# Second feed-forward's up-projection: weights as the moving operand, with a return path over VectorE transposes and SBUF to SBUF transfers

## Chip, cores and metric

One core of a Trainium2 chip. The metric is the device time of one execution in microseconds, as the median of three runs.

## What is computed

A sequence of 256 tokens of width 2048 goes through two transformer blocks, all in fp32. The change touches only the last part, the gated feed-forward of the second block, with 2 x 5632 hidden channels and a causal convolution of three taps over the tokens. Cut to what matters:

```
hn  = rms_norm(h, g2)                            # 256 x 2048
u   = hn @ w_up                                  # 256 x 11264: for each of 5632 channels a gate and a value
u   = w0*u[t-2] + w1*u[t-1] + w2*u[t]            # per channel, over tokens
a   = silu(u_gate) * u_value                     # 256 x 5632
out = h + rms_norm(a @ w_down, g3)               # 256 x 2048
```

## The kernel before

**Weights.** All weights of the program lie in one array `wstream` of 756 pieces. A piece is 512 KB, eight blocks of 128x128. SP loads them in order into a ring of four slots (`raw`); the load of piece i waits until the low part of piece i-4 has been made (`lo_ready`). Every product is made of three, for precision: a weight is split into a high part (ScalarE, `split_hi`, L1802, which waits until TensorE has used the piece four before it, `piece_used`) and a low part (VectorE, `split_lo`, L1100), and the activations have a high and a low part too (`A[:, k, 0]`, `A[:, k, 1]`; `H` likewise). High x high, high x low and low x high are summed in PSUM.

**Stages.** The second feed-forward runs in three chunks of 16, 16 and 12 tiles of 128 hidden channels (`CHUNKS2`). Each chunk has an up stage (`up0`, `up1`, `up2`: 64, 64 and 48 pieces) and a down stage (`dn0`, `dn1`, `dn2`: 32, 32 and 24 pieces). The stages follow each other without a break on TensorE; ScalarE and VectorE prepare pieces up to three ahead of it.

**Up stage.** The function `units` (L486, L494) takes four units (128 channels each; gate and value of two tiles) in turn. A weight block is the stationary operand. With its high part 512 columns go through (`A[:, k, :, :]`, both parts of 256 tokens), with its low part 256 columns. The result stands in PSUM with channels on partitions: 256 columns and 256 more, which VectorE adds up (`tensor_reduce`, L1131) into `z`, one unit every two pieces. GpSimd scales it by the norm's factor into `ub` (L2257), ScalarE makes the first tap (`c0`, L2207), VectorE the two others (`conv`, L1721 and L1724), ScalarE the sigmoid (L2213), GpSimd two products (L2341, L2347), ScalarE the high part of H (L2216), GpSimd the low part (L2352, `up_ready`). Within a chunk H tile i follows two units.

**Down stage.** In `down2` (L1059 to L1061) activations are stationary: for each of the tiles k and both halves of the tokens three matmuls of 512 columns, into two banks, one for each half. The four column groups f come one after another; each needs all H tiles.

**Opening of up0.** The norm ahead of up0 is made half by half: `turn_half` and `next_tiles` transpose tiles of x on TensorE (L958, L1014), ScalarE and VectorE make the parts of A (`a4_ready`, L1678, L1689), and the first two pieces are done by `half_piece` (L975, L981) for each token half by itself; `spread_rs` (L527) spreads the norm's factor over the partitions.

Of the kernel before, what the change touches and what calls it, by code (L numbers as in the profile page):

```python
# [26 lines left out]
P = 128  # L27
S = 256
# [43 lines left out]
for _c, _n in enumerate(CHUNKS2):  # L72
    STAGES += [(f"up{_c}", 2 * _n, 16), (f"dn{_c}", 8, _n)]
# [4 lines left out]
NZ = {"gate": 0, "wo": 0, "fd0": 0, "fd1": 0, "fd2": 0, "fd3": 0, "vs": 0, "cv": 0, "v2": 0, "misc": 1, "proj": 0, "wo2": 0, "dn0": 0, "dn1": 0, "dn2": 0}  # L78
_p = _u = _z = 0
for _name, _n, _k in STAGES:  # L80
    PB[_name], UB[_name], ZB[_name] = _p, _u, _z
    _blocks = _n * _k
    if _name in ("vs", "v2"):
        _blocks = _n // 2 * 4 * 16
    if _name[:2] in ROWS:
        _blocks = 16 * _k
    _p += 1 if _name == "misc" else _blocks // BLK
    _u += _n
    _z += NZ.get(_name, _n)
# [17 lines left out]


BY_TILE = tuple((k, k + 1) for k in range(12)) + ((12, 14, 0), (14, DT, 0), (12, 14, 2), (14, DT, 2))
# [43 lines left out]
ATT_PIECES = 32 + len(WO_FIRST)  # L153

# [39 lines left out]
def program(nc, xT, pT, wstream, consts, setup, params, grows, xrows, out):  # L194
# [11 lines left out]
    with ExitStack() as ctx:  # L206
# [47 lines left out]
        ub, c0 = ring(ptf, 0, 4, S + 4), ring(ptf, 4 * (S + 4), 2)  # L254
# [31 lines left out]
        mask = con[:, CO["mask"][0]:CO["mask"][1]]  # L286
        rs2b, rs3 = vN[:, QT, 0:S], vN[:, QT, S:2 * S]
# [61 lines left out]
        half_turned, post_half_hi, post_half_lo = sem("half_turned"), sem("post_half_hi"), sem("post_half_lo")  # L349
        up_c0, up_step, up_conv, up_sig, up_gated, up_h, up_hi, up_ready = (  # L350
# [71 lines left out]
        def _(sp):  # L422
# [11 lines left out]
            def load(i, s):  # L434
                sp.wait_ge(lo_ready, i - SLOTS + 1)
                sp.dma_start(raw[:, s, :], wstream[ds(i, 1)].rearrange("a p n -> p (a n)")).then_inc(raw_landed[s], 16)

            with sp.Fori(1, NPIECE // SLOTS - 1) as it:
                for j in range(SLOTS):
                    load(it * SLOTS + (SLOTS + j), j)  # L440
            for i in range(NPIECE // SLOTS * SLOTS, NPIECE):
                sp.wait_ge(lo_ready, i - SLOTS + 1)
                sp.dma_start(raw[:, i % SLOTS, :], wstream[i]).then_inc(raw_landed[i % SLOTS], 16)
# [10 lines left out]
        def _(pe):  # L454
# [74 lines left out]
            def rows_group(p, p0, u, u0, K, src, ready=None, between={}, upper=False):  # L529
# [4 lines left out]
                for k in range(K):  # L534
# [426 lines left out]
            def half_piece(q, t, js, between=None):  # L961

                p, tok = PB["up0"] + q, slice(t * P, t * P + P)
                pe.wait_ge(lo_ready, p + 1)
                blocks = [(k, j) for k in (2 * q, 2 * q + 1) for j in js]
                for k, j in blocks:
                    if t:
                        pe.wait_ge(a4_ready, k + 1)
                    else:
                        pe.wait_ge(post_half_lo, k + 1)  # L970
                        if k == 0:
                            pe.wait_ge(z_ready, UB["up0"] + j + 1)
                    i = (k % 2 * 4 + j) * P
                    bank = psum[(UB["up0"] + j) % 4][:, :].rearrange("p (h c) -> p h c", h=2)
                    nc.tensor.matmul(bank[:, :, tok], whi[:, p % SLOTS, i:i + P], A[:, k, :, tok], start=(k == t == 0), stop=False)  # L975
                if between:
                    between()
                for k, j in blocks:
                    i = (k % 2 * 4 + j) * P
                    bank = psum[(UB["up0"] + j) % 4][:, tok]  # L980
                    last = nc.tensor.matmul(bank, wlo[:, p % SLOTS, i:i + P], A[:, k, 0, tok], start=False, stop=False)  # L981
                if t:
                    last.then_inc(piece_used, 1)
# [40 lines left out]
            for q in range(2):  # L1024
                half_piece(q, 0, range(3))
            turn_half(1)
            for q in range(2):
                half_piece(q, 0, range(3, 4))
            half_piece(0, 1, range(4))
            half_piece(1, 1, range(4), between=lambda: next_tiles(0))  # L1030
# [3 lines left out]
            for c, n in enumerate(CHUNKS2):  # L1034
                up, dn = f"up{c}", f"dn{c}"

                def hidden2(it, **more):
                    units(it * 8 + PB[up], PB[up], it * 4 + UB[up], UB[up], 4, DT, lambda j, k: A[:, k, :, :],
                          lambda k: (a4_ready, k + 1), **more)
                if c == 0:  # L1040
                    late = {q: lambda q=q: next_tiles(q) for q in range(2, 6)}
# [4 lines left out]
                def down2(it, f):  # L1046

                    p = it * n + f * n // 2 + PB[dn]
                    s0 = PB[dn] + f * n // 2
                    u, u0 = it * 4 + 2 * f + UB[dn], 2 * f + UB[dn]  # L1050
                    for t in range(QT):
# [1425 lines left out]
```

## Time and profile before

| | us |
|---|---|
| runs, median of 3 | 2211.14 |
| runs, lowest and highest | 2210.64, 2211.28 |
| profiled execution, span | 2209.0 |
| TensorE busy | 2197.2 (99%) |
| VectorE busy | 1445.2 (65%) |
| ScalarE busy | 1106.9 (50%) |
| GpSimd busy | 550.7 (25%) |
| DMA, mean | 188 GB/s |

The span goes from the first to the last instruction of the profiled execution. Busy times of engines overlap each other. A matmul's shown duration (389 ns for 512 columns) is longer than the distance between two of them, since they are pipelined; the rate of TensorE is read from the starts in the timeline.

### The profile page before, as it was taken

To read this page: it belongs to the slowest core of one execution; us is meant where nothing else is said; L and a number is where in the kernel's file an instruction comes from. 1 tells how busy PE (TensorE), PEld (TensorE's weight loads), DVE (VectorE), ACT (ScalarE), POOL (GpSimd) and SP (SyncE) were. 2 spreads that over 40 slices of the span, in tenths; PEclk is the share of its full clock that TensorE was granted. 3 is DMA by queue.
4 is the path that set the end of the run, shared out by engine and by line. 5 is a ranking of instruction groups with operands and counts; after the bars stand their busy time and mean duration, and the time that the engine had idled before them with its cause. 6 is when DMAs were issued, how large, how long until landed. Compare 5 with 4: busy or idle time off the path is not lost.

```text
span 2209.0 us, 34195 instructions
## 1 busy us (share of the span) xinstructions
PE 2197.2 (99%) x11625; PEld 1878.9 (85%) x11625; DVE 1445.2 (65%) x1925; ACT 1106.9 (50%) x1654; POOL 550.7 (25%) x531
## 2 busy tenths in 40 slices
PE   9999999999999999999999999999999999999998
PEld 7888988888888888888888887888888888888887
DVE  6877765555664565555566667567785688756875
ACT  6445555453453454445455455565553455534553
POOL 3202220350240141053000033005540245403431
PEclk9999999999999999999999999999999999999999
DMA  7675335556555555556555653545555555555554
GB/s 254 232 230 163 115 128 204 170 190 208 191 190 192 189 189 192 186 192 193 187 185 179 227 171 135 193 160 188 195 188 196 192 183 192 189 195 192 186 209 149
DMA packets 118072, 414.21 MB, mean 188 GB/s; under 512 B 12896, under 2 KB 18048, under 8 KB 117472
## 3 DMA queue, kind: packets, MB, share of 16 engines
q1 hardware_dynamic: 111600, 401.37, 53.9%
q10 hardware_dynamic: 6384, 11.70, 1.7%
q8 instruction: 52, 0.85, 0.2%
q14 instruction: 36, 0.29, 0.0%
HBM read 409.29 MB, written 2.15 MB: 186 GB/s over the span
## 4 chain that ended last, share of the span: by engine, by line
PE 98%; DVE 1%; ACT 1%; issue 0%; DMA 0%; DVEq 0%; ACTq 0%
PE bank L486 33%; PE bank L494 17%; PE bank L543 7%; PE bank L545 7%; PE bank L544 7%; PE bank L1059 4%; PE bank L1060 4%; PE bank L1061 4%; PE bank L599 1%; PE bank L601 1%; PE bank L600 1%; PE bank L619 1%; PE bank L994 1%; PE bank L656 1%; PE bank L796 1%; PE bank L798 1%
## 5 line engine op out<-in xcount | busy, mean ns | idle before, releaser
L1100 DVE TENSOR_TENSOR wboth<-raw,wboth 128x1024 fp32r<-128x1024 f32 x756 | 982.2, 1302 | 607.8 <-ACT wboth L1802 607.1
L1802 ACT CAST wboth<-raw 128x1024 fp32r<-128x1024 f32 x756 | 790.9, 1049 | 711.5 <-PE bank L545 241.6
L486 PE MATMUL bank<-A,wboth 128*128 128x512 f32 x2928 | 705.1, 391 | 0.3 <-DVE wboth L1100 0.3
L486 PEld LDWEIGHTS bank<-A,wboth 128*128 128x128 f32 x2928 | 537.0, 188 | 104.6 <-issue 1.0
L494 PEld LDWEIGHTS bank<-A,wboth 128*128 128x128 f32 x2928 | 376.7, 191 | 14.8
L494 PE MATMUL bank<-A,wboth 128*128 128x256 f32 x2928 | 384.0, 283 | 0.0
L543 PE MATMUL bank<-wboth,H 128*128 128x512 f32 x576 | 224.6, 390 | 0.0
L545 PE MATMUL bank<-wboth,H 128*128 128x512 f32 x576 | 224.2, 389 | 0.0
L544 PE MATMUL bank<-wboth,H 128*128 128x512 f32 x576 | 224.1, 389 | 0.0
L2257 POOL TENSOR_TENSOR bias<-z,rs 128x256 f32<-128x256 f32 x64 | 75.7, 1182 | 481.2 <-DVE z L1131 391.6
L2257 POOL TENSOR_TENSOR PT<-z,rs 128x256 f32<-128x256 f32 x88 | 73.4, 835 | 465.4 <-DVE z L1131 464.8
L1131 DVE TENSOR_REDUCE z<-bank 128x256 f32<-128x512 f32 x172 | 118.2, 688 | 41.1 <-PE bank L486 40.8
L1059 PE MATMUL bank<-wboth,H 128*128 128x512 f32 x352 | 136.9, 389 | 0.0
L1060 PE MATMUL bank<-wboth,H 128*128 128x512 f32 x352 | 136.9, 389 | 0.0
L1061 PE MATMUL bank<-wboth,H 128*128 128x512 f32 x352 | 136.9, 389 | 0.0
L545 PEld LDWEIGHTS bank<-wboth,H 128*128 128x128 f32 x576 | 108.1, 188 | 22.6
L543 PEld LDWEIGHTS bank<-wboth,H 128*128 128x128 f32 x576 | 108.1, 188 | 22.3
L544 PEld LDWEIGHTS bank<-wboth,H 128*128 128x128 f32 x576 | 108.1, 188 | 22.2
L2347 POOL TENSOR_TENSOR bias<-Sm 128x256 f32<-128x256 f32 x44 | 70.0, 1592 | 37.9 <-DVE Sm L1724 37.7
L486 PE MATMUL bank<-H,wboth 128*128 128x512 f32 x320 | 79.1, 394 | 0.0
L2010 ACT ACTIVATE Sm<-bias 128x256 f32<-128x256 f32 x64 | 26.8, 418 | 102.6 <-POOL bias L2257 102.6
L1061 PEld LDWEIGHTS bank<-wboth,H 128*128 128x128 f32 x352 | 66.1, 188 | 13.8
(293 smaller groups left out, 2409.1 us busy)
## 6 DMA issues: line engine op xcount, KB each, us to landing
raw<-wstream SPq DMA_DIRECT2D x756, 512.0 KB, 3.3
bias<-bias_rows ACTq DMA_DIRECT2D x6, 512.0 KB, 5.4
x<-xrows ACTq DMA_DIRECT2D x1, 2048.0 KB, 10.0
bias<-grows ACTq DMA_DIRECT2D x2, 1024.0 KB, 6.1
out<-x SPq DMA_DIRECT2D x8, 256.0 KB, 2.1
x<-xT SPq DMA_DIRECT2D x7, 256.0 KB, 4.6
pA<-bias_rows ACTq DMA_DIRECT2D x2, 512.0 KB, 8.9
Sm<-grows ACTq DMA_DIRECT2D x1, 1024.0 KB, 5.8
```

The source lines that it names most:

```text
L486: last = nc.tensor.matmul(bank(j)[:, :], whi[:, s, cols(i)], moving(j, k), start=(k == 0), stop=(k == K - 1))
L494: last = nc.tensor.matmul(bank(j)[:, 0:S], wlo[:, s, cols(i)], moving(j, k)[:, 0, :], start=False, stop=False)
L543: nc.tensor.matmul(bank[:, :], src[:, k, 0, tok], whi[:, s, w], start=(k == 0), stop=False)
L544: nc.tensor.matmul(bank[:, :], src[:, k, 0, tok], wlo[:, s, w], start=False, stop=False)
L545: last = nc.tensor.matmul(bank[:, :], src[:, k, 1, tok], whi[:, s, w], start=False, stop=(k == K - 1))
L1059: nc.tensor.matmul(bank[:, :], H[:, k, 0, tok], whi[:, s, w], start=(k == 0), stop=False)
L1060: nc.tensor.matmul(bank[:, :], H[:, k, 0, tok], wlo[:, s, w], start=False, stop=False)
L1061: return nc.tensor.matmul(bank[:, :], H[:, k, 1, tok], whi[:, s, w], start=False, stop=(k == n - 1))
L1100: V.tensor_tensor(wlo[:, s, :], raw[:, s, :], whi[:, s, :].bitcast(F32), ALU.subtract).then_inc(lo_ready, 1)
L1131: V.tensor_reduce(dst(j) if dst else z[:, (z0 + j) % 4, :], bank[:, :].rearrange("p (h c) -> p c h", h=2), AX, ALU.add).then_inc(z_ready, 1)
L1802: C.copy(whi[:, s, :], raw[:, s, :]).then_inc(hi_ready, 1)
L2257: return lambda zz: G.tensor_tensor(dst, zz, by, ALU.mult)
```

## The change

In up stages the activations become the stationary operand and 512 columns of weights (four units) the moving one; the code is the existing `rows_group`. A group of four units takes eight pieces, and its result stands in two banks with tokens on partitions and 4 x 128 channels in the columns. To bring it back to channels on partitions, VectorE transposes each bank in blocks of 32x32 into `flip` (`up_flip`; the buffer of `z`), which keeps each block in its quarter of 32 partitions, and 16 transfers of 32 partitions x 1 KB on the SP queue carry the blocks from quarter i to quarter j (`carry`, into `land`, two buffers in `kT`). GpSimd reads `land`, scales and writes `ub` as before. The taps, products and splits of a group of four come at fixed places of the piece order (`TAP_AT`, `CONV_AT`, `GATE_AT`, `HIGH_AT`), 12 to 16 pieces after the group's first piece. In SP's order the six, five and five transfers of a group stand ahead of three successive loads (`CARRY`, `LOADED`).

In the down stages the pieces of the first two column groups are interleaved (`dn_first`): all but the last two of f=0, then all but the last two of f=1, then the two last of each. The weight stream is laid out accordingly. The opening of up0 uses `half_tiles`, tile by tile for each half. Loops over up and down stages are written out.

```
-    STAGES += [(f"up{_c}", 2 * _n, 16), (f"dn{_c}", 8, _n)]
+    STAGES += [(f"up{_c}", _n, 16), (f"dn{_c}", 8, _n)]
+LOADED = 7
+TAP_AT, GATE_AT, HIGH_AT = (12, 12, 13, 13), (13, 14), (15, 16)
+CONV_AT = (12, 12, 13, 14)
+CARRY = [range(0, 6), range(6, 11), range(11, 16)]
+def dn_first(n):
+    return [(f, h) for f in range(2) for h in range(n // 2 - 2)] + [(f, h) for f in range(2) for h in (n // 2 - 2, n // 2 - 1)]
+        flip = z[:, :, :].rearrange("p a b -> p (a b)")
+        land = [kT[:, i, :, :].rearrange("p a b -> p (a b)")[:, 0:8 * P] for i in range(2)]
...
+            def carry(src, dst, steps_of, landed):
+                for step in steps_of:
+                    i, j = divmod(step, 4)
+                    sp.dma_start(dst[32 * j:32 * j + 32, 256 * i:256 * i + 256],
+                                 src[32 * i:32 * i + 32, 256 * j:256 * j + 256]).then_inc(landed, 16)
+            def up_carry(c, m, steps_of):
+                if 0 in steps_of:
+                    sp.wait_ge(z_ready, 4 + UB[f"up{c}"] + 2 * m + 2)
+                    if c or m >= 2:
+                        sp.wait_ge(z_used, 4 + ZB[f"up{c}"] + 4 * m - 4)
+                carry(flip, land[m % 2], steps_of, up_landed)
+            done = BLK
+            for c, n in enumerate(CHUNKS2):
+                p = PB[f"up{c}"] + LOADED
+                loads(done, p)
+                for i in range(4 * n + 4):
+                    for step, part in enumerate(CARRY):
+                        if i - step >= 8 and (i - step) % 8 == 0:
+                            up_carry(c, (i - step) // 8 - 1, part)
+                    load(p + i, (p + i) % SLOTS)
...
+            half_tiles((0, 1), 0)
+            half_tiles((2,), 0)
             turn_half(1)
+            half_tiles((3,), 0)
+            half_tiles((0, 1), 1)
+            half_tiles((2,), 1)
+            next_tiles(0)
+            half_tiles((3,), 1)
             next_tiles(1)
...
-                    hidden2(0, mixed=1, first=BY_TILE, begin=2, halved=(6,), between={**late, NORM_AT["up0"]: lambda: spread_rs(3)})
-                with pe.Fori(1 if c == 0 else 0, n // 2) as it:
-                    hidden2(it)
+                for m in range(n // 2):
+                    rows_group(PB[up] + 8 * m, PB[up] + 8 * m, UB[up] + 2 * m, UB[up] + 2 * m, DT, A, lambda k: (a4_ready, k + 1), late,
+                               begin=4 if c == m == 0 else 0)
...
+                for i, (f, h) in enumerate(dn_first(n)):
+                    dn_piece(PB[dn] + i, f, h)
...
+            def up_flip(c, m):
+                dve.wait_ge(piece_used, PB[up] + SLOTS + 8 * m + 8)
+                if c or m:
+                    dve.wait_ge(up_landed, 64 * (ZB[up] - ZB["up0"] + 4 * m))
+                for t in range(QT):
+                    V.transpose(flip.rearrange("p (j t d b) -> p t d j b", j=4, t=QT, d=4)[:, t, :, :, :],
+                                psum[(UB[up] + 2 * m + t) % 4][:, :].rearrange("p (d j a) -> p d j a", d=4, j=4)).then_inc(z_ready, 1)
...
+                for m in range(n // 2):
+                    pool.wait_ge(up_landed, 64 * (ZB[up] - ZB["up0"] + 4 * m + 4))
+                    for j in range(4):
+                        preact(4 * m + j)
+                    for i in (2 * m, 2 * m + 1):
+                        gated(i)
+                        product(i)
+                    for i in (2 * m, 2 * m + 1):
+                        product_lo(i)
```

## Rows read from the trace of the kernel before

**Rows 1.** The page's first line: span of the profiled execution.
```profile
span 2209.0 us, 34195 instructions
```

**Rows 2.** The page's chain of work that ended last, by engine.
```profile
PE 98%; DVE 1%; ACT 1%; issue 0%; DMA 0%; DVEq 0%; ACTq 0%
```

**Rows 3.** Windows: busy time of each engine in up1.
```profile
core 0: us, PE busy (x) PEld busy (x) DVE busy (x) ACT busy (x) POOL busy (x), PEclk, DMA share, GB/s
1737.00:1915.00 178.00, 178.00 (x1025) 157.33 (x1024) 144.66 (x159) 94.31 (x126) 83.39 (x76) 1.00 0.55 187
```

**Rows 4.** Timeline of TensorE, up0 and start of dn0: start, duration, instruction, count.
```profile
1559.03 3.82 PE L486 MATMUL bank<-A,wboth 128*128 128x512 f32 x16
1562.68 2.08 PE L494 MATMUL bank<-A,wboth 128*128 128x256 f32 x16
1564.60 3.82 PE L486 MATMUL bank<-A,wboth 128*128 128x512 f32 x16
...
1648.09 2.00 PE L486 MATMUL bank<-A,wboth 128*128 128x512 f32 x8
1649.93 0.39 PE L1059 MATMUL bank<-wboth,H 128*128 128x512 f32 x1
```

**Rows 5.** Timeline of TensorE: first matmuls of up1.
```profile
1736.97 1.98 PE L486 MATMUL bank<-A,wboth 128*128 128x512 f32 x8
```

**Rows 6.** Source line L543, gate stage: duration ns min/median/max, first and last start.
```profile
L543 PE MATMUL bank<-wboth,A x128: 389/389/476, 1112.5 to 1202.5; 128*128 128x512 f32 x128
```

**Rows 7.** Timeline of TensorE in the opening of up0.
```profile
1464.64 0.87 PE L975 MATMUL bank<-A,wboth 128*128 128x256 f32 x6
...
1486.21 0.60 PE L1014 MATMUL bank<-con,x 128*128 128x128 f32 x4
...
1489.94 0.70 PE L527 MATMUL bank<-acc,ones 128*128 128x256 f32 x2 [0.33 <-DVE acc L1190]
```

**Rows 8.** Timeline of VectorE in the opening of up0.
```profile
1466.65 0.75 DVE L1673 SCALAR_TENSOR_TENSOR x<-y,small,x 128x512 f32<-128x512 f32 x1
...
1470.59 1.22 DVE L1100 TENSOR_TENSOR wboth<-raw,wboth 128x1024 fp32r<-128x1024 f32 x1
1471.73 0.74 DVE L1673 SCALAR_TENSOR_TENSOR x<-y,small,x 128x512 f32<-128x512 f32 x1
1472.88 0.88 DVE L1678 SCALAR_TENSOR_TENSOR A<-bank,par,A 128x256 fp32r<-128x256 f32 x2 [0.41 <-ACT A L2140]
```

**Rows 9.** Groups by line in up1, dn1 and up2; last, source line L2257.
```profile
L1100 DVE TENSOR_TENSOR wboth<-raw,wboth 128x1024 fp32r<-128x1024 f32 x144 | 196.1, 1362 | 78.2 <-ACT wboth L1802 78.2
L1802 ACT CAST wboth<-raw 128x1024 fp32r<-128x1024 f32 x144 | 151.4, 1052 | 128.0 <-PE bank L1061 51.7 <-PE bank L494 45.0 <-PE bank L486 31.3
L1721 DVE SCALAR_TENSOR_TENSOR Sm<-PT,par 128x256 f32<-128x256 f32 x55 | 40.1, 729 | 0.0
L1131 DVE TENSOR_REDUCE z<-bank 128x256 f32<-128x512 f32 x55 | 38.0, 691 | 17.9 <-PE bank L486 17.9
L1724 DVE SCALAR_TENSOR_TENSOR Sm<-PT,par,Sm 128x256 f32<-128x256 f32 x55 | 26.7, 485 | 2.0
...
L2257 POOL TENSOR_TENSOR PT<-z,rs x88: 732/740/1785, 1493.3 to 2136.7; 128x256 f32<-128x256 f32 x88
```

**Rows 10.** Source line L1745: copy of 512 PSUM columns on VectorE.
```profile
L1745 DVE COPY y<-bank x8: 680/686/694, 1672.0 to 1737.9; 128x512 f32 x8
```

**Rows 11.** Transfers: issues by line, KB, us to landing; durations of two issues, ns.
```profile
raw<-wstream SPq DMA_DIRECT2D x756, 512.0 KB, 3.3
out<-x SPq DMA_DIRECT2D x8, 256.0 KB, 2.1
vT<-vT ACTq DMA_DIRECT2D x1, 256.0 KB, 5.4
...
L436 SPq DMA_DIRECT2D raw<-wstream x748: 332/333/823, 17.2 to 2179.3; - x187
L1972 ACTq DMA_DIRECT2D vT<-vT x1: 487/487/487, 166.8 to 166.8; - x1
```

More of the change, by code:

```diff
@@ L86 @@
         _blocks = 16 * _k
+    if _name[:2] == "up":
+        _blocks = 2 * _n * _k
     _p += 1 if _name == "misc" else _blocks // BLK
@@ L435, in load, with loads @@
                 sp.wait_ge(lo_ready, i - SLOTS + 1)
[L436 to L443, printed above, removed]
+                piece = wstream[i] if isinstance(i, int) else wstream[ds(i, 1)].rearrange("a p n -> p (a n)")
+                sp.dma_start(raw[:, s, :], piece).then_inc(raw_landed[s], 16)
+            def loads(a, b):
+                with sp.Fori(a // SLOTS, b // SLOTS) as it:
+                    for j in range(SLOTS):
+                        load(it * SLOTS + j, j)
+                for i in range(b // SLOTS * SLOTS, b):
+                    load(i, i % SLOTS)
+            def carry(src, dst, steps_of, landed):
[18 more added lines that the diff above has]
+                    load(p + i, (p + i) % SLOTS)
+                done = p + 4 * n + 4
+            loads(done, NPIECE)
             for t in range(QT):
@@ L533, in rows_group @@
                         pe.wait_ge(z_ready, u + t + 1)
-                for k in range(K):
+                for k in range(begin, K):
                     if ready:
@@ new lines, in _ @@
+                for i in range(n, 2 * n):
+                    if n == CH or i < 3 * n // 2 + FIN_SPLIT // 2:
+                        dn_piece(PB[dn] + i, 2 * i // n, i % (n // 2))
+                t0 += n
+            p = PB["dn2"] + 3 * n // 2
+            for t in range(QT):
+                for k in range(FIN_SPLIT, n):
+                    pe.wait_ge(lo_ready, p + k // 2 + 1)
+                    last = rows_of(p + k // 2, 3, k, t)
+                    if t and k % 2:
+                        last.then_inc(piece_used, 1)
+                if t == 0:
+                    last.then_inc(dn_half, 1)
@@ new lines, in down2_in @@
+            def down2_in(c, f):
+                dn, n = f"dn{c}", CHUNKS2[c]
+                last = dn_first(n).index((f, n // 2 - 1)) if f < 2 else n // 2 * f + n // 2 - 1
+                dve.wait_ge(piece_used, PB[dn] + SLOTS + last + 1)
+                for t in range(QT):
+                    dst = yN[:, t, f * WIDE:f * WIDE + WIDE]
+                    bank = psum[(UB[dn] + 2 * f + t) % 4][:, :]
+                    if c == 0:
+                        V.tensor_copy(dst, bank).then_inc(z_ready, 1)
+                    else:
+                        V.tensor_tensor(dst, dst, bank, ALU.add).then_inc(z_ready, 1)
@@ L2431 @@
     for n in CHUNKS2:
-        stream += [ordered(both[t0:t0 + n].reshape(2 * n, DT, P, P), 1 if t0 == 0 else 0, first=BY_TILE), rows(down[t0 * P:(t0 + n) * P])]
+        wide = both[t0:t0 + n].reshape(n // 2, 4, DT, P, P).transpose(0, 2, 1, 3, 4).reshape(-1, P, P)
+        stream += [wide, rows_out(down[t0 * P:(t0 + n) * P], dn_first(n))]
         t0 += n
```

239 lines of the change are left out of this document (89 added, 150 removed).

## Prediction

> **What bounds the kernel now.** I read the chain that ended last first: 98% of the span is TensorE [rows 2]. The windows by stage say the same of the second feed-forward: in the 178 us of up1 TensorE is busy for all 178, VectorE for 145, ScalarE 94, GpSimd 83, at a granted clock of 1.00 and a DMA share of 0.55 [rows 3]. So only two things can move the time here: what TensorE takes for a piece of weights, and new waits of TensorE. The timeline gives the first. In a regular up stage two pieces (16 wide matmuls of 512 columns, 16 narrow ones of 256) repeat; the block at 1559.03 comes again at 1564.60, and the sixteenth repeat starts at 1648.09: 89.06 us for 32 pieces, 2.783 us a piece [rows 4]. Inside it the wide run starts at 1559.03 and the narrow one at 1562.68, 3.65/16 = 0.228 us a wide one; 1562.68 to 1564.60 is 0.120 us a narrow one. Half the columns cost more than half the time, by about 6 ns here, so each matmul carries some 13 ns that its columns don't explain. A down stage has 12 matmuls of 512 columns a piece, activations stationary: dn0 starts at 1649.93, up1 at 1736.97, 87.04 us for 32 pieces, 2.720 us a piece [rows 4, 5].
>
> **Part 1, the matmuls.** Per piece the old up stage streams 8x512 + 8x256 = 6144 columns in 16 matmuls, the new one 12x512 = 6144 in 12. The columns are equal; four matmuls fewer at 13 to 16 ns are the 0.063 us between 2.783 and 2.720. I price a new up piece at the down stage's 2.720, since its loop is `rows_group`, the code that also runs the gate stage with A as the stationary operand; there a matmul shows the same 389 ns [rows 6] as in the down stages. Up1 and up2 have 64 + 48 = 112 pieces: 112 x 0.0631 = 7.1 us off, all of it on the path.
>
> Up0 has 64 pieces in 1464.64 to 1649.93 = 185.29 us [rows 4, 7]. Its last seven groups, 56 pieces, become 152.3 us. The first group has to be laid out step by step, as it is fed by the norm, whose VectorE and ScalarE work isn't changed. TensorE does three tiles of token half 0, 3 x 0.68 = 2.04 us, to 1466.7, then wants the transposes of half 1; the VectorE step that they read (the one at 1466.65, 0.75 long) ends at 1467.4 [rows 8]: 0.7 us of waiting that is new, because the old code had 2.8 us of matmuls ahead. Then 0.4 of transposes, tile 3, and tiles 0 to 2 of half 1 to 1470.6, as the halves arrive from 1468.5 on; transposes 0.35, tile 3, transposes 0.35, to 1472.05. Tile 4 needs a weight split at 1470.59 (1.22), an add at 1471.73 (0.74) and a 0.44 us low part: ready at 1472.9 [rows 8], a second wait of 0.85. Pieces 2 to 5 and three sets of transposes bring TensorE to 1484.8; the fourth set starts there. In the trace that set starts at 1486.21 and the matmul that spreads the norm's factor at 1489.94 [rows 7], 3.73 later, all VectorE and ScalarE. The same 3.73 gives 1488.6, while TensorE is done with piece 6 at 1487.9: a third wait of 0.7. Then 0.35 + 2.72: group 0 ends at 1491.6, 27.0 us. Up0 is 27.0 + 152.3 = 179.3, 6.0 us less. The down stages keep their matmuls, only reordered: 0.
>
> **Part 2, from PSUM back to channels on partitions.** Four reductions a group of 8 pieces (691 ns each) go; two 512-column transposes come, which no row shows. Nearest is the copy of 512 PSUM columns, 0.69 us [rows 9, 10]; as the low end I take 0.35 (a half), as the high end the 1.36 us of a 1024-column split, since a strided write could be slow. VectorE then has, a group, 8 x 1.36 + 4 x (0.73 + 0.49) + 2 x 0.69 = 17.1 us of TensorE's 21.8; 18.5 at the high end. It is not the bound, and its two transposes are back to back where four reductions were spread, so one low part comes 1.4 us later; three split pieces (8.2 us) lie ahead of TensorE then. The price is 0, beyond this cover the excess.
>
> **Part 3, sixteen 32 KB transfers a group on SP.** This queue also issues the weight loads. What is queued behind: the first six transfers wait for the transposes, and behind them stands the load of piece 8m+15; five more stand before 8m+16, five before 8m+17. An issue takes 0.333 us; one of ScalarE, from SBUF to SBUF, 0.487 [rows 11]. Let E be the end of a group on TensorE. Transposes done at E+1.4, six issues to E+3.6, the load, five issues; the next load waits for the low part of piece 8m+12, at E + 2.72 + 1.05 + 1.36 = E+5.1; the last five are out at E+7.3 to E+8. TensorE wants piece 8m+15 at E+19.0, and its high and low part take 1.05 + 1.36 [rows 9], so the first must start by E+16.6, and the load, 3.3 us from issue to landing [rows 11], must go by E+13: 9 us of cover. The loads behind it have as much. The last transfer lands 2.1 us (out from x) to 5.4 us (SBUF to SBUF, 256 KB) after its issue [rows 11], at E+10 to E+13. ScalarE looks for it after the high part of piece 8m+15, at E + 4 x 2.72 + 1.05 = E+12, holding only splits that TensorE wants by E+21.8, so it may be late until about E+16. GpSimd's four scalings (740 to 1785 ns each [rows 9]) run behind it. Price 0; 22 x the excess beyond E+16. The bytes: 512 KB more for every 4 MB, so the share of 0.55 goes to 0.62, or 0.68 if 1 KB rows cost double; no bound.
>
> The Trainium skill (DMA: Bandwidth & Descriptors, section on measured HBM to SBUF transfers) says that transfers below 64 KB are dominated by their descriptors, and speaks against this. Its 0.95 us of DMA time at 64 KB would, if the sixteen were served one after another, make an estimate of 15 us, to E+16.6, stall every group by 0.6 us and bring the time back to 2211; no run here shows it. The mechanism is rival (b) below.
>
> **Part 4, the seams.** The last group's H comes late: gate and copy are placed 13 to 16 pieces after the group's start, the last convolution runs behind the low part of piece 8m+17 (E + 6 x 2.72 + 2.41 = E+18.7) to about E+20.5, the product to E+22, ScalarE's last copy behind the split of piece 8m+19 (E+22.8) to E+23.2, and GpSimd's two low parts are done at about E+23.5 and, at 0.74 to 1.79 each, E+24 to E+25.6. The reordered down stage asks for it at its piece 13 (E+35) with 16 tiles and at piece 9 (E+24.5, second tile E+25.9) with 12: no wait in chunks 0 and 1; in chunk 2 0 to 1.5 us, I take 0. Without the reordering all three seams would stall, by 6 us (piece 7, E+19) or 11 us (piece 5, E+13.6). The tail behind the last matmul isn't touched.
>
> **Sum.** 6.0 + 7.1 = 13.1 us. Span 2209.0 [rows 1] - 13.1 = 2195.9. The median of the runs lies 2.1 above the span; this adds to 2198.0. Bounds: without the three waits of group 0, 2195.8; with 1.5 us at the seam and a group 0 no shorter than before, 2202.
>
> **Rivals.** (a) The return path is late by a little in each group (slow scatter of the transposes, 32 KB transfers landing at E+17 or so): 0.1 to 0.4 us x 22 takes back 2 to 9 us, 2200 to 2207. Against it: 3 us of cover even at the 5.4 us landing. (b) Slower than before, by one mechanism: the transfers are served in series in the queue, each holding the next. At 2.1 us each [rows 11] sixteen end at E+35, 19 us past the deciding point of E+16, and 22 groups lose some 400 us; it decides from (16 - 1.4)/16 = 0.9 us a transfer, and at 1.0 us it costs 22 x 1.4 = 31 us: 2229. Against it: the eight output transfers at the end are issued closer than their 2.1 us landing and still show 2.1 to 2.2 each, so they overlap. (c) The change doesn't do what it says, as the 0.063 us belongs to the mixture of high and low parts and not to the count: then up pieces stay at 2.78 and the time at 2211. The gate stage speaks against it. (d) Group 0 is better than laid out, with no waits: 2196.
>
> **How the numbers follow.** Forecast 2198.0, from 2195.5 to 2201: 0.70, with (d) inside. (a) 0.14, of which 0.03 ends within 0.2% (4.4 us, about what a measurement of this kernel can tell from no change). (b) 0.08; (c) 0.05; better than 2195.5, 0.03. Faster 0.70 + 0.11 + 0.03 = 0.84, same 0.08, slower 0.08. The range 2195.0 to 2205.5 holds the forecast and most of (a).
>
> **What would show it.** Right: up stages at 2.72 us a piece (174.1 us for up1, 130.6 for up2), no TensorE waits beyond some 2 us in group 0, transposes near 0.7 us, the last transfer landed by E+13. Wrong: TensorE idle before the first or second piece pair of each group, released by a split (path late), or before dn2's tenth piece, released by H. The prediction falls with any recurring wait above 0.3 us a group.

## The result and the profile after

| | before | after |
|---|---|---|
| median of the runs, us | 2210.89 (4 runs, 2210.46 to 2211.28) | 2260.05 (4 runs, 2258.52 to 2262.86) |
| ratio, 95% interval | | 1.0223 [1.0211, 1.0236] |
| profiled execution, span, us | 2209.0 | 2258.8 |

The change makes the kernel 2.2% slower; the forecast was 2198.0 and the range ended at 2205.5. One execution of e7 below took 2719.8 us at a mean granted clock of 0.752, and no figure counts it. The page's first line, and its chain of work that ended last, by engine (before: [rows 1, 2]):

```profile
span 2258.8 us, 32069 instructions
...
PE 73%; DVE 13%; SPq 7%; DMA 3%; POOL 2%; issue 1%; ACT 1%; DVEq 0%; ACTq 0%; POOLq 0%
```

TensorE held 98% of that chain; now it holds 73%, and VectorE, SP's queue, transfers and GpSimd appear in it together. So the path leaves TensorE and runs through several engines, which is what a loop looks like. Windows of up0 and up1 (columns as in [rows 3]):

```profile
1505.00:1645.00 140.00, 128.42 (x545) 103.76 (x545) 95.73 (x105) 64.74 (x95) 62.90 (x59) 0.98 0.56 190
1740.00:1915.00 175.00, 167.28 (x725) 136.47 (x725) 109.06 (x113) 74.73 (x98) 54.22 (x50) 0.99 0.57 189
```

TensorE is idle for 11.6 and 7.7 us of them, yet VectorE, ScalarE and GpSimd are less busy than before and the DMA share is as it was: none of them is the bound by its own work. TensorE's waits from up0 to the end of dn2 (engine, line, releaser: us in total, times, longest):

```profile
PE bank L582 <- DVE wboth L1119: 27.4, 13, 3.2
PE bank L1080 <- issue: 7.0, 3, 3.0
PE bank L1080 <- DVE wboth L1119: 5.4, 3, 2.7
PE bank L1080 <- POOL H L2384: 4.7, 1, 4.7
```

From the fourth group of each chunk on, one wait stands ahead of each group's first piece (5, 5 and 3), and two more follow in each down stage (6); the last row is dn2's tenth piece. In 19 of the 20 TensorE waits for a low part of weights (L1119), not for the return path itself; the three put down to "issue" end 0.10 us after such a split does (1663.98, then 1664.08). The timeline of TensorE shows one, and what follows a longer one:

```profile
1586.98 0.39 PE L584 MATMUL bank<-wboth,A 128*128 128x512 f32 x1
1588.84 0.47 PE L582 MATMUL bank<-wboth,A 128*128 128x512 f32 x1 [1.47 <-DVE wboth L1119]
...
1565.88 0.63 PE L582 MATMUL bank<-wboth,A 128*128 128x512 f32 x1
1566.31 0.63 PE L583 MATMUL bank<-wboth,A 128*128 128x512 f32 x1
```

The lower two rows lie 0.43 us apart where 0.227 is usual: behind the 3.1 us wait that ended at 1563.72 the granted clock is 0.50 (1.2 GHz) for a while. There are five such stretches, at waits of 3.0 to 4.7 us, together 20.5 us, of which TensorE works for 19.2 and so loses 9.6; before has none in these stages. But inside a chunk this is no cost of its own: with 1.7 us lost behind 1563.72 the next wait ends 25.1 us later and is 1.5 us; without such a loss, from 1613.15 to 1638.53, it ends 25.4 us later and is 3.2. Something else sets the 25 us.

The loop itself is read from one turn of the chain, 1594 to 1618. First SP's timeline, then the chain (start, us, what):

```profile
1595.37 3.68 SPq L462 DMA_DIRECT2D kT<-z  x6
1599.09 0.58 SPq L448 DMA_DIRECT2D raw<-wstream  x1
1599.71 3.05 SPq L462 DMA_DIRECT2D kT<-z  x5
1602.81 0.59 SPq L448 DMA_DIRECT2D raw<-wstream  x1
1603.44 3.04 SPq L462 DMA_DIRECT2D kT<-z  x5
```

```profile
1594.12 1.22 DVE z L1755 x2
...
1605.89 1.84 DMA kT<-z
1607.79 0.75 POOL PT L2367
1608.57 0.52 ACT vN L2230
1609.63 0.84 DVE Sm L1743
...
1614.75 1.14 DVE wboth L1119
1615.89 0.89 DVE Sm L1740
1617.20 1.22 DVE wboth L1119
1618.42 1.24 DVE z L1755 x2
```

Transposes at 1594, sixteen issues and two loads between them on SP to 1606.5, landing, scaling on GpSimd at 1607.8, tap on ScalarE, four convolutions (L1740, L1743) with the splits between them on VectorE, and behind these, since VectorE works in order, the transposes of the next group. Over all groups the first half (the trip, from the start of the transposes to the start of the scaling) takes 13.8 to 15.1 us, 14.3 at the median, and the second, to the next transposes, 10.5 to 10.8. A turn is 24.9 us on average (25.1 in up0, 24.8 in up1 and up2; 24.3 to 25.6), against TensorE's 8 x 2.72 = 21.76. (The texts of e6 and e12 below reckon with 14.6 and 10.7, some 0.4 us too much in all.) What the loop takes too much, TensorE waits for, because the splits stand in the same VectorE queue behind convolutions that aren't ready.

Two source lines give the sizes (ns min/median/max; the issue, and the transposes), and one the landing:

```profile
L462 SPq DMA_DIRECT2D kT<-z x352: 507/591/1704, 1494.7 to 2192.4; - x176
...
L1755 DVE STREAM_TRANSPOSE z<-bank x44: 673/692/717, 1493.4 to 2181.0; 128x512 f32<-128x512 f32 x44
```

```profile
kT<-z SPq DMA_DIRECT2D x352, 32.0 KB, 2.3
```

What an issue takes goes by what was issued just before it. A weight load on an idle queue takes 0.33 us, as before the change, but the two loads between the transfers take 0.58 and 0.59; a transfer right behind a load takes 0.507, right behind another transfer 0.591. So the stretch on SP is eighteen issues, 11.1 us.

### The profile page after: what moved, and what is told of

It reads as the page before. It is cut to its first block, busy times and chain, and to the rows that moved or that the text cites. A ratio compares the mean times of both kernels' runs of the same rounds, so it can differ in the third digit from the quotient of the medians.

```text
span 2258.8 us, 32069 instructions
## 1 busy us (share of the span) xinstructions
PE 2201.1 (97%) x10889; PEld 1843.1 (82%) x10889; DVE 1425.9 (63%) x1881; ACT 1093.8 (48%) x1654; POOL 549.6 (24%) x531
## 4 chain that ended last, share of the span: by engine, by line
PE 73%; DVE 13%; SPq 7%; DMA 3%; POOL 2%; issue 1%; ACT 1%; DVEq 0%; ACTq 0%; POOLq 0%
PE bank L525 18%; PE bank L533 10%; PE bank L584 8%; PE bank L582 8%; PE bank L583 8%; DVE wboth L1119 6%; SPq L462 6%; DVE Sm L1740 3%; PE bank L1080 3%; PE bank L1082 3%; PE bank L1081 3%; DVE Sm L1743 2%; DMA kT<-z 2%; SPq L448 1%; DVE z L1755 1%
## 5 line engine op out<-in xcount | busy, mean ns | idle before, releaser
L1119 DVE TENSOR_TENSOR wboth<-raw,wboth 128x1024 fp32r<-128x1024 f32 x756 | 966.0, 1286 | 624.8 <-ACT wboth L1825 624.1
L525 PE MATMUL bank<-A,wboth 128*128 128x512 f32 x1536 | 371.3, 392 | 0.0
L582 PE MATMUL bank<-wboth,A 128*128 128x512 f32 x824 | 325.7, 395 | 27.8 <-DVE wboth L1119 27.4
L525 PEld LDWEIGHTS bank<-A,wboth 128*128 128x128 f32 x1536 | 281.6, 188 | 54.3
L584 PE MATMUL bank<-wboth,A 128*128 128x512 f32 x824 | 322.7, 392 | 0.0
L583 PE MATMUL bank<-wboth,A 128*128 128x512 f32 x824 | 322.7, 392 | 0.0
L582 PEld LDWEIGHTS bank<-wboth,A 128*128 128x128 f32 x824 | 155.7, 189 | 67.5 <-issue 36.0
L533 PEld LDWEIGHTS bank<-A,wboth 128*128 128x128 f32 x1536 | 197.9, 191 | 7.9
L533 PE MATMUL bank<-A,wboth 128*128 128x256 f32 x1536 | 202.4, 283 | 0.0
L2367 POOL TENSOR_TENSOR PT<-kT,rs 128x256 f32<-128x256 f32 x88 | 72.0, 849 | 510.9 <-DMA kT<-z 510.9
L584 PEld LDWEIGHTS bank<-wboth,A 128*128 128x128 f32 x824 | 155.9, 189 | 33.2
L583 PEld LDWEIGHTS bank<-wboth,A 128*128 128x128 f32 x824 | 155.9, 189 | 31.6
L1080 PE MATMUL bank<-wboth,H 128*128 128x512 f32 x352 | 140.0, 398 | 17.2 <-issue 7.0
L584 PEld LDWEIGHTS bank<-wboth,H 128*128 128x128 f32 x576 | 108.1, 188 | 22.4
L583 PEld LDWEIGHTS bank<-wboth,H 128*128 128x128 f32 x576 | 108.1, 188 | 22.3
```

Source lines behind the costliest of these rows:

```text
L525: last = nc.tensor.matmul(bank(j)[:, :], whi[:, s, cols(i)], moving(j, k), start=(k == 0), stop=(k == K - 1))
L533: last = nc.tensor.matmul(bank(j)[:, 0:S], wlo[:, s, cols(i)], moving(j, k)[:, 0, :], start=False, stop=False)
L582: nc.tensor.matmul(bank[:, :], src[:, k, 0, tok], whi[:, s, w], start=(k == 0), stop=False)
L583: nc.tensor.matmul(bank[:, :], src[:, k, 0, tok], wlo[:, s, w], start=False, stop=False)
L584: last = nc.tensor.matmul(bank[:, :], src[:, k, 1, tok], whi[:, s, w], start=False, stop=(k == K - 1))
L1080: nc.tensor.matmul(bank[:, :], H[:, k, 0, tok], whi[:, s, w], start=(k == 0), stop=False)
```

## The experiments

The theory, L: the turn of the loop (trip plus the VectorE work that stands ahead of the next transposes) is longer than TensorE's 21.76 us, and its main term is sixteen issues at 0.62 us. The first rival, Q: the issues hold up the weight loads behind them. Further rivals are in each expectation. All ratios are to runs of the kernel before on the same chip; the chips differ between experiments, and the kernel before took 2210.7 to 2211.4 us on them. All trips are counted as above.

### e1: nobody reads the transferred blocks

```
+                    dve.wait_ge(z_used, 4 + ZB[up] + 4 * m)
...
-                    landed = land[j // 4 % 2].rearrange(...)
+                    landed = flip.rearrange(...)
-                    pool.wait_ge(up_landed, 64 * (ZB[up] - ZB["up0"] + 4 * m + 4))
+                    pool.wait_ge(z_ready, 4 + UB[up] + 2 * m + 2)
```

> All sixteen transfers of a group are still issued in the same places of SP's queue, but nobody reads what they carry: GpSimd scales from the transposed buffer itself as soon as the transposes are done (so the blocks stand in the wrong quarters and the output isn't the reference's). Only the next transposes still wait for the transfers' landing. Theory L (a loop: transposes of group m, 16 issues on SP at 0.6 us, landing, scaling, convolution, which stand ahead of the transposes of group m+1 in VectorE's queue; 24.3 us a turn against TensorE's 21.8): the loop is open, no TensorE wait recurs by group, up stages at 2.72 us a piece, time 2197 to 2203. Theory Q (the weight loads are late because some 10 us of issues stand ahead of them in SP's queue, whoever reads the transfers): TensorE keeps its wait of 2 to 3 us a group, time 2250 to 2262.

2199.81 (2 runs), ratio 0.9949 [0.993, 0.9969]; span 2197.7. All 352 transfers are still issued ahead of the same loads, and no group waits: besides the three waits of group 0 there is one of 0.41 us at dn2's tenth piece. So neither the queue's load (Q) nor the bytes cost anything; it is the waiting for the path. This run also measures part 1 alone: up1 from first to last takes 174.08 us, up2 130.56, as forecast.

### e2: taps, convolutions, sigmoids and high parts four pieces later

```
+def group_at(i, at, n):
+    last = n // 2 - 1
+    if i == 8 * last + at:
+        return last
+    m, rest = divmod(i - at - 4, 8)
+    return m if rest == 0 and 0 <= m < last else None
-                        m = (i - CONV_AT[j]) // 8
+                        m = group_at(i, CONV_AT[j], n)
... (likewise for taps, sigmoids and high parts on ScalarE, the high parts now first)
```

> Taps, convolution, gates and high copies of every group but the last of a chunk are placed four pieces later, behind the transposes of the next group in VectorE's queue; transfers and SP's order unchanged. Theory L: the transposes of group m+1 no longer wait for group m's transfers, no wait recurs by group; only the seam into dn2 may keep about 3 us (H asked for at E+24.5, there at about E+27); time 2198 to 2206, and with the granted clock at full after the opening. Theory Q: as with the change, 2250 to 2262.

2204.43 (10 runs), ratio 0.9969 [0.9959, 0.9978]; span 2203.4. The trip is as long as before (13.8 to 15.7 us), but the transposes no longer stand behind the convolutions of the group before, and they start every 21.76 us. Beyond group 0 only dn2's tenth piece waits:

```profile
PE bank L1091 <- POOL H L2395: 3.4, 1, 3.4
```

Fifty-six microseconds come back from an edit that touches no transfer: the cost was the order in which things wait, not work.

### e3: the same trip by way of HBM, one write and four reads

```
-                for step in steps_of:
-                    i, j = divmod(step, 4)
-                    sp.dma_start(dst[32 * j:32 * j + 32, 256 * i:256 * i + 256], src[32 * i:32 * i + 32, 256 * j:256 * j + 256])...
+                if 0 in steps_of:
+                    sp.dma_start(turned[dst].ap(), src).then_inc(rows_out, 16)
+                elif 6 in steps_of:
+                    up_written[0] += 16
+                    sp.wait_ge(rows_out, 16 + up_written[0])
+                    for j in range(4):
+                        sp.dma_start(land[dst][32 * j:32 * j + 32, :]..., <column block j of turned[dst]>)...
```

> Sixteen transfers of 32 KB become one of 512 KB out to a buffer in HBM and four of 128 KB back: five issues and one landing waited for in SP's queue. Theory L: from the transposes to the last landing 8 to 10 us in place of 13.8, so a turn of the loop is 19 to 20.5 us, below TensorE's 21.8: no wait by group, 2198 to 2205. Theory Q also expects the loads on time, 2198 to 2205. If it is the landing of small transfers that costs and not their issue, HBM twice is as slow as before: 2240 or more.

2204.85 (10 runs), ratio 0.9975 [0.9965, 0.9984]; span 2201.7. Here the order is untouched and the trip shortened. One trip on VectorE, SP and GpSimd:

```profile
1603.05 1.31 DVE L1760 STREAM_TRANSPOSE z<-bank 128x512 f32<-128x512 f32 x2
...
1604.38 0.33 SPq L462 DMA_DIRECT2D turned<-z  x1
1605.54 0.98 SPq L449 DMA_DIRECT2D raw<-wstream  x1
1609.56 1.77 SPq L467 DMA_DIRECT2D kT<-turned  x4
...
1613.73 3.79 POOL L2372 TENSOR_TENSOR PT<-kT,rs 128x256 f32<-128x256 f32 x4 [7.63 <-DMA kT<-turned]
```

From the transposes to the scaling 9.8 to 11.5 us, 10.8 at the median (longer than the 8 to 10 expected) and 12.7 in the last group; with the second half of the loop 10.8 + 10.55 = 21.4 a turn, just under 21.76, and no group waits. Twice the bytes, by way of HBM, five issues instead of sixteen, and the trip is 3.5 us shorter. One wait of 3.2 us is left, again at dn2's tenth piece, with 3.4 us at half clock behind it.

### e4: eight further transfers of 8 KB a group

```
+                    if step % 2:
+                        sp.dma_start(spare[32 * j:32 * j + 32, 64 * i:64 * i + 64], src[32 * i:32 * i + 32, 256 * j:256 * j + 64]).then_inc(landed, 16)
-                    pool.wait_ge(up_landed, 64 * ...)
+                    pool.wait_ge(up_landed, 96 * ...)
```

> Eight further transfers a group of 8 KB each (32 rows of 256 B, to a spare place), between the sixteen; GpSimd and VectorE wait for all 24. Theory L, with the price per issue and not per byte: 8 x 0.6 = 4.8 us more a turn of the loop, some 20 to 22 turns: 2260 + 95 to 106, so 2350 to 2366. If the price goes by bytes, an eighth of the data costs under 1 us a turn: 2265 to 2280.

2370.2 (2 runs), ratio 1.072 [1.0699, 1.0742]: 110 us more than the changed kernel, 4 above the 95 to 106 expected; over 22 groups 5.0 each, or 8 x 0.62. The trip is 19.1 us at the median, the turn 29.8 on average, 4.9 more than with sixteen. The issues of the small transfers:

```profile
L466 SPq DMA_DIRECT2D vN<-z x176: 507/591/1701, 1496.3 to 2304.9; - x176
```

A quarter of the bytes in as many rows, and the same 591 ns: the price is one of the issue, not of the bytes. Whether it goes by the 32 rows isn't shown.

### e5: late places and HBM together

The edits of e2 and e3.

> Both mends together: five issues by way of HBM, and taps and convolution behind the next transposes. The loop is open and the last group's blocks land about 10.5 us after the transposes. Theory L with the seam as a term of its own: no wait by group, the wait at dn2's tenth piece falls from 3.4 us to 0 to 1 us, and the granted clock stays at full through it; 2197.5 to 2201, below both kernels. If the seam's wait doesn't depend on the landing it stays at 3 us: 2203 to 2206.

2203.11 (5 runs), ratio 0.9966 [0.9952, 0.9979]; span 2201.3. The expectation was missed: no group waits, but dn2's tenth piece still does, by 3.4 us. The trip of the last group shows why (ScalarE's queue, SP, GpSimd):

```profile
2124.38 0.35 ACTq L2277 DMA_DIRECT2D bias<-grows  x1
...
2125.58 0.33 SPq L473 DMA_DIRECT2D turned<-z  x1
...
2134.59 1.77 SPq L478 DMA_DIRECT2D kT<-turned  x4
...
2139.04 2.39 POOL L2383 TENSOR_TENSOR PT<-kT,rs 128x256 f32<-128x256 f32 x3 [0.28 <-DMA kT<-turned]
```

The load of the gain row for the output (1 MB) is issued 1.2 us ahead of the last group's write. From write to reads it takes 9.0 us here, and 4.15 in the middle of up0 (1603.34 to 1607.49). So the late part of the trip looks like the large load's doing; e8 puts it to the test.

### e6: half of the sixteen transfers

From the third group on, eight of the sixteen are left out, so the blocks that they carry are missing from the result.

```
+                    if not every and (i + j) % 2:
+                        continue
```

> From the third group of up0 on, eight of the sixteen transfers of a group are left out (the other eight bring what they brought before; the rest of the buffer keeps old values, so the output isn't the reference's). Everything else as with the change. Theory L: 8 x 0.62 = 5.0 us less, transposes to scaling 14.6 -> 9.7 us, a turn 25.3 -> 20.4 us, below TensorE's 21.8: no wait by group after the first two, 2200 to 2208 with the seam's 3 us. If the turn were set by something else than the issues, the wait by group would stay: 2240 or more.

2202.86 (5 runs), ratio 0.9965 [0.9953, 0.9978]; span 2201.0. The trip is 13.9 and 15.0 us in the two groups with sixteen, 9.6 to 10.7 with eight (9.8 at the median; 11.5 in the last): 4.5 less than the changed kernel's 14.3, where 8 x 0.62 = 5.0 was expected. One wait of 1.7 us behind the two full groups, then none in the up stages, and 1.7 at dn2's tenth piece.

### e7: eight issued by SP, eight by ScalarE's queue

```
+                    if i % 8 in (0, 1) and 8 <= i <= 4 * n + 1:
+                        m = i // 8 - 1
+                        if i % 8 == 0:
+                            act.wait_ge(z_ready, 4 + UB[up] + 2 * m + 2)
+                        for step in (range(8, 12), range(12, 16))[i % 8]:
+                            ...act.dma_start(land[m % 2][...], flip[...]).then_inc(up_landed, 16)
```

> Sixteen transfers as with the change, eight issued by SP, eight by ScalarE in two lots of four behind its splits; order of all else unchanged. Theory L: the two queues issue at the same time, transposes to scaling about 9 to 11 us, a turn 20 to 21.8 us: most of the wait by group goes, 2200 to 2215. If issues of two queues take turns at one place, so that sixteen still cost 16 x 0.6, nothing is gained: 2255 to 2265.

2204.43 (5 runs), ratio 0.9968 [0.9955, 0.998]; span 2203.2. All sixteen transfers are there, and the trip is 9.2 to 10.9 us, 9.5 at the median (13.5 in the last group). Both queues in one group:

```profile
1603.86 2.41 SPq L462 DMA_DIRECT2D kT<-z  x4
...
1603.86 2.71 ACTq L2260 DMA_DIRECT2D kT<-z  x4
```

They issue side by side at 0.6 to 0.68 us each, so the serial step is each queue's own, not a shared one. The Trainium skill (DMA: Bandwidth & Descriptors, section Issuing engines are not separate DMA queues) says that issuing from several engines saves only the time on the sequencer, "usually small relative to the DMA itself". The first half agrees with the 4.9 us that the trip lost, eight issues' worth; the second doesn't hold for this pattern: sixteen issues are 10 us on one queue, beside a landing of 2.3. ScalarE pays: in the group shown it does no work from 1602.5 to 1606.6, 1.4 us waiting for the transposes and 2.7 issuing. The seam keeps a wait of 3.4 us.

### e8: e5 with the gain row loaded earlier

```
-                        if i == 4 * n:
+                        if i == 16:
                             act.dma_start(g3row, grows[2]...)
```

> As the fifth kernel (five issues by way of HBM, convolution late), and the 1 MB load of the last gain row (bias<-grows, issued by ScalarE at the first piece of dn2, as the blocks of the last group are on their way) moved to piece 16 of up2, where nothing hurries. If that load delays the last transfers: from transposes to scaling at the seam 14.8 -> about 10.5 us, the wait at dn2's tenth piece 3.4 -> 0 to 0.6 us, time 2198.5 to 2201. If it has no part in it: 3.4 us stay, 2202.5 to 2205.

2203.73 (5 runs), ratio 0.9962 [0.9948, 0.9975]; span 2201.9. The collision is gone (write to reads 4.55 us instead of 9.0), but the wait only fell from 3.4 to 2.4 and the time not at all. With the late places GpSimd is still at the low parts of the group before when the blocks land, and begins the scaling at 2138.35 right behind them. One cause removed, a second stood right behind it. The 2.4 us are between the two forecasts (0 to 0.6, and 3.4).

### e9: e7's two queues with late places and the early gain row

> Sixteen SBUF to SBUF transfers, eight each from SP's and ScalarE's queue, convolution late, the gain row's load moved as in the eighth kernel: no trip through HBM. From transposes to scaling 9.5 to 10 us in the seventh kernel, so the seam closes as well: wait 0 to 0.6 us, 2198.5 to 2201.5; with the load's collision as the only cause of the seam's wait it must close here too, if the load has no part in it 3.4 us stay and 2203 to 2205 come out.

2208.07 (10 runs), ratio 0.9985 [0.9976, 0.9995]; span 2207.2. Missed: no group waits by more than 0.63 us, but the seam got worse, 4.7 us. In nearly every group the scaling now starts 17.2 us after the transposes, behind GpSimd's work of the group before, and in the last group at 2143.48. That ScalarE's own issues push this work back is a reading of the timeline and not shown by a run.

### e10: e3 with the gain row loaded earlier

> The return path as in the run by way of HBM (one write of 512 KB, four reads of 128 KB), with the fixed places of the changed kernel for taps, products and splits (not the late ones), and the 1 MB load of the gain row g3 issued at piece 16 of up2 instead of behind its last piece. In the run with the late places GpSimd came to the last group's scaling without having been idle, because the previous group's work stood there; here that work ends 8 us earlier. Theory (the last 3 us at dn2's tenth piece are the gain row's load beside the last group's trip, once GpSimd is free): write to reads 4.2 to 4.6 us there, scaling 10.5 us after the transposes instead of 12.7, the wait at dn2's tenth piece 0 to 0.8 instead of 3.2, no half clock behind it, 22 loop turns of 21.3 to 21.8 us: 2198.5 to 2201. Rival (the order of convolution and splits on VectorE sets it, the load has no part): scaling earlier, but the wait still 2 to 3 us, 2203 to 2205.

2200.83 (5 runs), ratio 0.9951 [0.9938, 0.9965]; span 2200.8. Half right. The last trip is 9.65 us (12.7 in e3), the write to the reads 3.7, and there is no half clock. The wait stayed:

```profile
PE bank L1085 <- POOL H L2389: 2.8, 1, 2.8
```

The last transposes start at 2128.04, 3.9 us behind dn2's first matmul (2124.16); in e1 it is 0.2 (2123.92 and 2123.72). Ahead of them on VectorE:

```profile
2125.51 0.96 DVE L1745 SCALAR_TENSOR_TENSOR Sm<-PT,par,vN 128x256 f32<-128x256 f32 x1
2126.51 0.48 DVE L1748 SCALAR_TENSOR_TENSOR Sm<-PT,par,Sm 128x256 f32<-128x256 f32 x1
2126.91 1.22 DVE L1124 TENSOR_TENSOR wboth<-raw,wboth 128x1024 fp32r<-128x1024 f32 x1
2128.04 1.31 DVE L1760 STREAM_TRANSPOSE z<-bank 128x512 f32<-128x512 f32 x2
```

Much of that lateness is the moved load's own. It is now issued just ahead of the second group's write (ScalarE's queue, then SP):

```profile
2039.17 0.35 ACTq L2266 DMA_DIRECT2D bias<-grows  x1
...
2039.79 0.33 SPq L462 DMA_DIRECT2D turned<-z  x1
...
2048.41 1.77 SPq L467 DMA_DIRECT2D kT<-turned  x4
```

From write to reads it takes 8.6 us there (3.8 in e3's second group), and the next transposes start 24.8 us after this group's. A loop of 21.4 us under a pace of 21.76 makes up only some 0.4 us a turn, so the last transposes are still late, by 3.9 us against 2.1 in e3. The collision was moved from the last group to the second, not removed. No group waits for it; the seam does. What e10 takes with the load out of every trip's way wasn't run.

### e11: e10 with two convolutions behind the next transposes

```
+BEHIND = {("conv", 2): 15, ("conv", 3): 15, ("gate", 1): 16, ("high", 1): 17}
                     if i % 8 == 7 and i < 4 * n:
                         up_flip(c, i // 8)
+                        for j in (2, 3):
+                            m = group_at(i, "conv", j, n)
+                            if m is not None:
+                                conv(2 * t0 + 4 * m + j, j)
```

> The run before (return path by HBM, gain row at piece 16) left a wait of 2.8 us at dn2's tenth piece, although the last trip took 9.65 us: the last transposes started at 2128.0, 4.1 us later than in the run in which nobody waits for the transfers (2123.9), since the third and fourth convolution of the group before stand ahead of them on VectorE. Here these two convolutions (and with them one sigmoid and one high part on ScalarE, at 16 and 17) come right behind the transposes of the next group, except in the last group of a chunk. Theory (a trip and the work that stands ahead of the next transposes add up round the loop): transposes 2.5 to 3 us earlier throughout, at E+1.4 to E+2 instead of E+4.5, trip still 9.7 to 11, scaling of the last group at about 2135, wait at dn2's tenth piece 0 to 0.8, time 2198 to 2200. Rival (the last group's own convolutions and splits set it): wait still 2 to 3 us, 2200.5 to 2202.

2200.54 (5 runs, 2199.72 to 2201.99), ratio 0.9954 [0.994, 0.9967]; span 2197.8. TensorE's waits from the opening of up0 to the end of dn2, all of them:

```profile
PE bank L1098 <- POOL H L2406: 0.9, 1, 0.9
PE bank L1015 <- DVE x L1710: 0.6, 1, 0.6
PE bank L600 <- DVE A L1715: 0.6, 1, 0.6
PE bank L584 <- DVE acc L1227: 0.4, 1, 0.4
```

The last transposes start at 2123.58, the scaling at 2134.93, as expected; the wait is 0.9 (0 to 0.8 was expected). The second group meets the gain row's load here too (a trip of 14.8 us, 23.7 to the next transposes), but the next turn takes 19.8 and all is made up. The profiled span is 3.0 below e10's, but e11's profile is of its fastest run and e10's of its slowest: the medians and ratios can't be told apart, and e11's median lies 0.5 above the 2198 to 2200 expected, at the lower end of the rival's range.

### e12: e11's order with the sixteen transfers

> The same order on VectorE and ScalarE and the gain row at piece 16, but with the sixteen transfers of the changed kernel on SP, unchanged. This is a middle point for the law of the loop. Changed kernel: 14.6 us from transposes to scaling and 10.7 from there to the next transposes, 25.3 against TensorE's 21.76. Two convolutions (2 x 1.45 us) leave the second part, none of the first: 14.6 + 7.8 = 22.4 us a turn, 0.6 us too much, so a wait of some 0.6 us in nearly every group (10 to 14 us in all, too short for stretches at half clock), and about 5 us at dn2's tenth piece, where the last trip is 4 us longer than by HBM: 2212 to 2220. Rival (a wait comes from the 16 issues holding up the weight loads, and the order on VectorE is no matter): waits of 2 us as in the changed kernel, 2250 or more; second rival (only work on GpSimd and the transfers count, the late convolutions just displace the wait): 2230 to 2245.

2222.74 (5 runs), ratio 1.0055 [1.0041, 1.0069]; span 2222.4. The transposes start 23.0 us apart on average (22.2 to 24.2), the trip is 14.5, the second half of the turn 8.5. The waits:

```profile
PE bank L595 <- DVE wboth L1132: 8.7, 9, 1.5
PE bank L1093 <- POOL H L2401: 4.7, 1, 4.7
PE bank L1093 <- issue: 2.4, 3, 1.3
```

A turn of 22.4 was expected and 2212 to 2220; it is 23.0, as the second half is 8.5 us and not 7.8, and the time is 3 us above. Both rivals (2230 and more) are further off. With 29.8, 24.9, 23.0 and 21.4 us a turn (the last held back to 21.76 by TensorE) the kernel takes 2370, 2260, 2223 and 2201 to 2205 us: the time follows the excess over 21.76, and below it the loop costs nothing but its seam.

## Why the prediction was wrong, point by point

**The step that failed** is in part 3, and it is a way of reckoning. Each wait was held against a due time counted from E, the end of a group on TensorE, and each had slack: the last transfer out at E+8 and landed by E+10 to E+13, "it may be late until about E+16". But the transposes of the next group stand, in VectorE's order, behind the convolutions of this one, and these wait for the transfers. Counted round, it is a loop with a period of its own, and the sum to make was: 1.3 + issues + landing + scaling, tap, four convolutions and the splits between them. Even with the forecast's own 0.333 us an issue it comes to about 24.9 - 16 x (0.62 - 0.333) = 20.3 us, 1.5 us under 21.76: where the text saw 3 to 9 us of cover there was 1.5. The loop decides from about 0.62 - 3.1/16 = 0.43 us an issue. These two are estimates from the rows above. e2 shows the order to be the cause (56 us back with the trip unchanged), e3, e6 and e7 the trip (3.5 to 4.9 us shorter, and no waits by group; e6 has one behind its two full groups).

**The term that was mis-sized** is the issue: 0.333 us was taken from the weight load on the same queue [rows 11], while these transfers take 0.591, spaced 0.62 to 0.63, and the loads between them 0.58; the row beside it, ScalarE's 0.487 from SBUF to SBUF, was quoted and not used, though it lies above the 0.43 from which the loop decides. The last is issued 12 us behind the start of the transposes, where the text has 7 to 8. The landing (2.3 us, 2.1 to 5.4 forecast) was right.

**Rival (a)** had the right mechanism ("late by a little in each group") and a size of 0.1 to 0.4 us; the 19 recurring waits are 0.7 to 3.2 us, 2.1 on average. Its chance of 0.14 and its upper end, 2207, both rested on the slack from E. **Rival (b)** put the serial step into the transfers and its deciding point at 0.9 us each. The transfers do overlap, as argued from the output's; the serial step is the issue, and 0.6 us sufficed, since the loop decides and not E+16. The Trainium skill (DMA: Bandwidth & Descriptors, section on measured HBM to SBUF transfers) calls transfers below 64 KB dominated by their descriptors. The direction agrees, with sixteen of 32 KB costing more than five larger ones (e3), but the estimate that the prediction made of the page's 0.95 us, in series, gave 2211, and by another mechanism. Here the landings overlap, and e4 shows 8 KB and 32 KB at one price on the issuing queue, which the rule doesn't speak of.

**Right steps.** (1) 2.720 us a piece: 174.08 and 130.56 us for up1 and up2 in e1, 7.1 us less. (2) The opening: waits of 0.6, 0.4 and 0.37 us where 0.7, 0.85 and 0.7 were laid out; dn0 starts at 1645.0 in e1, 4.9 us earlier than before, 6.0 forecast: group 0 was some 1 us longer than counted. (3) The transposes, 0.692 us as the copy [rows 10], at no price. (4) The bytes are no bound: e3 moves more at a share of 0.70. (5) No wait in chunks 0 and 1 from H, and dn2's tenth piece as the one seam: 0.4 us with no return path to wait for (e1), 4.7 in the changed kernel; 0 was taken and 1.5 set as the bound. The sum of these was 2198.0; the runs without the loop's excess give 2199.8 (e1) and 2200.5 (e11).

**The account.** Span forecast 2195.9, measured 2258.8, 62.9 us more. 47.8 are TensorE's idle time in 20 places beyond group 0, counted from the distances of its matmuls; 9.6 are lost at half clock behind the longer of them; some 4 are slower matmuls in the first two pieces behind each wait (2.8 to 2.9 us a piece instead of 2.72); 1.4 lie ahead of group 1, 0.5 of them a later start of up0. This says where the time lies, not what it is due to: idle time, slow clock and slow pieces fill up the same turn of 25 us.

## What to carry to other kernels

Where work goes from one in-order engine through others and back to the first, add up the whole turn and hold it against the period of the bound; slack at each wait by itself says nothing, and a turn just below the period still arrives late where the stage ends. If the turn is too long, look first at what stands ahead of its start in the first engine's order: moving that took no work away and gave back 56 us (e2), though what is moved back can be missed at the end of the stage (e8). Count transfers on a queue by number as well as by bytes, take the issue's duration from the nearest form of transfer and from issues that follow each other, and look what large load is issued just before a small one that someone waits for.

## What the runs showed of the hardware

- The issue of a transfer of 32 partitions from SBUF to SBUF takes 0.591 us on SP right behind another, for 32 KB and for 8 KB alike (changed kernel, e4), and 0.507 behind a weight load. A weight load of 512 KB to 128 partitions takes 0.33 on an idle queue, 0.43 right behind another load and 0.58 right behind such a transfer; one write of 512 KB to HBM takes 0.327, a read of 128 KB into 32 partitions 0.43 behind another (e3).
- Two queues issue such transfers at the same time (e7): eight and eight make the trip 9.5 us instead of 14.3.
- From SBUF by way of HBM back to SBUF, 512 KB in one write and four reads, scaling starts 9.8 to 11.5 us after the transposes; the write lands after 4.2 at the median (e3). Beside a load of 1 MB issued 0.6 to 1.2 us before it, write to reads went to 9.0 us in e5, 8.6 in e10 and 7.1 in e3.
- TensorE's granted clock fell to half (1.2 GHz) at five waits of 3.0 to 4.7 us in the changed kernel, at the seam at waits of 2.4 (e8) to 4.7 us (e12), and at every wait of e4 behind group 0, the shortest 2.3 us; it did not at 2.6 us in the changed kernel (2125.63), at 2.8 in e10 and at 3.4 in e5. Inside the loop it cost nothing, as the next wait was shorter by as much; at the last seam it may: e2 and e5 have the same wait of 3.4 us there, e2 with the half clock (1.7 us lost) and 2204.4, e5 without it and 2203.1.
